# Stage borders, first loads and closing rows of a two-block transformer kernel, changed together

## The reference

```python
def reference(x, c, ctx, ...):
    x = first_block(x, c, ctx, ...)        # attention + mLSTM mixer, then 16 experts
    return second_block(x, c_2, ctx_2, ...)  # two layers

# first_block: x = x + g1 * mixer(modulate(rmsnorm(x)))    8-head latent attention, a bidirectional mLSTM
#              x = x + g2 * ec_moe(modulate(rmsnorm(x)))   each expert takes 128 tokens; scatter-add
#              return rmsnorm(x, final_norm)
# _layer of second_block, for l in (0, 1):
shift, scale, gate = split(silu(c) @ w_mod + b_mod, 3)
h  = _rmsnorm(x, norm_g) * (1 + scale) + shift
parts = _split_cols(h @ w_in)              # q, k, v, gates, Fourier, convolution and pooling inputs
o_att = silu(parts[3]) * _latent_attention(q, k, v, kc, vc)   # 4 query heads, 2 key heads of width 64
out = concatenate([o_f, o_att, o_c, o_p]) @ w_out
x_new = x + gate * out                     # the context rows too, in layer 0
```

## Time and profile before

| | |
|---|---|
| median of 3 runs | 3560.42 us (3559.0 to 3563.74) |
| the profiled execution | 3564.75 us |
| its span, first to last instruction | 3563.0 us |
| PE busy | 3214.0 us, 90% |
| DVE / ACT / POOL busy | 52% / 40% / 20% |
| mean granted PE clock | 0.946 of full |

### The profile page before, as it was taken

The page is one execution under the profiler, slowest core; times in us unless marked ns, Lnnn a source line. Parts: engine busy times, 40 slices in busy tenths (PEclk is TensorE's granted clock), DMA queues, the critical chain, the costliest instruction groups (busy, mean ns, idle before and its releaser), DMA issues. The chain is left out here.

```text
span 3563.0 us, 43053 instructions
## 1 busy us (share of the span) xinstructions
PE 3214.0 (90%) x17109; PEld 2595.1 (73%) x17109; DVE 1852.6 (52%) x2501; ACT 1413.5 (40%) x1941; POOL 695.1 (20%) x460
## 2 busy tenths in 40 slices
PE   7989998999999799793999999599988996998989
PEld 3867775778778677673878787488877775887867
DVE  4366785444444354646788888434416443152643
ACT  4222231433333244432777777431116434212640
POOL 2200001011111255200455555220001003000100
PEclk7999999999999899896999999799999997999999
DMA  6426555001000231324999999421112134211122
GB/s 200 117 80 209 182 170 184 31 24 44 24 26 24 59 116 58 131 103 184 359 378 388 379 389 372 143 66 52 38 34 54 48 113 154 61 43 44 48 72 83
DMA packets 247250, 470.72 MB, mean 132 GB/s; under 512 B 23936, under 2 KB 135673, under 8 KB 247053
## 3 DMA queue, kind: packets, MB, share of 16 engines
q1 hardware_dynamic: 231304, 410.09, 33.4%
q0 software_dynamic: 15264, 57.70, 4.9%
q10 hardware_dynamic: 484, 0.15, 0.0%
HBM read 405.34 MB, written 55.22 MB: 129 GB/s over the span
## 5 line engine op out<-in xcount | busy, mean ns | idle before, releaser
L2558 DVE TENSOR_TENSOR exp_wl<-wts_raw,exp_wh 128x2048 fp32r<-128x2048 f32 x144 | 394.3, 2773 | 105.9 <-ACT exp_wh L2518 105.9
L2518 ACT ACTIVATE exp_wh<-wts_raw 128x2048 fp32r<-128x2048 f32 x192 | 368.0, 1919 | 196.5 <-PE exp_gate L2447 64.1
L2724 PE MATMUL pr_ps<-l_h_high,pr_wh 128*128 128x512 f32 (+1 forms) x896 | 335.1, 374 | 0.0
L2725 PE MATMUL pr_ps<-l_h_low,pr_wh 128*128 128x512 f32 (+1 forms) x896 | 329.6, 368 | 0.0
L2726 PE MATMUL pr_ps<-l_h_high,pr_wl 128*128 128x512 f32 (+1 forms) x896 | 329.0, 367 | 0.0
L2417 POOL TENSOR_TENSOR exp_wl<-wts_raw,exp_wh 128x2048 fp32r<-128x2048 f32 x48 | 229.4, 4780 | 265.0 <-ACT exp_wh L2518 265.0
L842 PE MATMUL in_ps<-iw_h_high,in_wh 128*128 128x512 f32 (+1 forms) x696 | 268.7, 386 | 0.0
L843 PE MATMUL in_ps<-iw_h_low,in_wh 128*128 128x512 f32 (+1 forms) x696 | 263.8, 379 | 0.0
L844 PE MATMUL in_ps<-iw_h_high,in_wl 128*128 128x512 f32 (+1 forms) x696 | 263.3, 378 | 0.0
L2886 DVE TENSOR_TENSOR pr_wl<-pw_raw,pr_wh 128x512 fp32r<-128x512 f32 x84 | 57.7, 691 | 333.4 <-ACT pr_wh L2804 332.1
L1067 DVE SCALAR_TENSOR_TENSOR g_scratch<-g_scratch,g_c 128x512 f32<-128x512 f32 x240 | 181.8, 785 | 19.8 <-DVE g_scratch L1067 12.7
(11 more groups left out here) (515 smaller groups left out, 7222.8 us busy)
## 6 DMA issues: line engine op xcount, KB each, us to landing
wts_raw<-in_w_e_gate SPq DMA_DIRECT2D x64, 1024.0 KB, 9.6
wts_raw<-in_w_e_up SPq DMA_DIRECT2D x64, 1024.0 KB, 8.8
wts_raw<-in_w_e_down SPq DMA_DIRECT2D x64, 1024.0 KB, 7.6
g_scratch<-in_w_mod SPq DMA_DIRECT2D x80, 512.0 KB, 4.6
pw_raw<-in_w_in SPq DMA_DIRECT2D x88, 256.0 KB, 2.9
iw_raw<-in_w_in SPq DMA_DIRECT2D x74, 256.0 KB, 4.6
mod_w<-in_w_mod SPq DMA_DIRECT2D x4, 2048.0 KB, 11.7
wo_w<-in_w_out SPq DMA_DIRECT2D x2, 4096.0 KB, 13.6
```

The lines of the kernel that those rows point to most:

```text
L2518: act.activation(wh[:, m % RING], raw[:, m % RAW_RING], ACT.Copy).then_inc(high, 1)
L2558: dve.tensor_tensor(wl[:, m % RING], raw[:, m % RAW_RING], wh[:, m % RING].bitcast(F32), ALU.subtract).then_inc(low, 1)
L2724: nc.tensor.matmul(out, wh[:, slot, k, :], hi, start=h == 0 and k == 0, stop=False)
L2725: nc.tensor.matmul(out, wh[:, slot, k, :], lw, start=False, stop=False)
```

## The change

- `Phase` takes a phase `to`. With it, its semaphores are handed on and neither cleared nor followed by a barrier at its end. A carrier phase `g.carry` collects them; they are cleared where iw, mli, mw, pw0, pw1 and wo1 end. A new phase `two` around both layers holds the weights ring, its semaphores and those of `project_out`'s stores. mod, iw, mli, mw, pw0, pw1 and wo1 still end with a clearing and a barrier.
- All Blocks are opened with `no_gpsimd_drain=True`.
- `project_first`: two row buffers used in turn; five quarters a tile at first and four from the 70th, so that block 19 falls to the last tile instead of behind it; the gates are copied, turned and added three to five tiles after `xm` 7, inside the loop, in the buffer `kr`.
- `FinalRows`: context rows in two loads; x1 before the table; the first weights are issued by ACT, which waits for the last scatter first.
- `project_in`: ACT rounds the keys after tiles 17 and 18, DVE takes their rests after 19 and 20, POOL zeroes the other half; they lie in a buffer that `attention_2` uses directly.
- `attention_2`: SP only prefetches the Fourier operands. Queries are rounded from `parts` for two row tiles at a time (three ACT and two DVE instructions), the first pair ahead of the loop, the next in each second unit. POOL has no list any more.
- `project_out`: the last tile is multiplied and finished by column halves; a tile's norm comes ahead of the preparation of later tiles; SP issues the next layer's first four half tiles of weights at the end of its list; with a normed copy POOL doesn't wait for the stores.
- `TurnedRows` with loads: SP loads row by row tile, each behind the store of that tile, the 7th and later ones behind all stores of xb; ACT and DVE start behind all stores.

```diff
 class Phase(ExitStack):
+    def __init__(self, nc, tag, to=None):
     def __exit__(self, *exc):
         if exc[0] is None:
-            self.nc.clear_and_free_semaphores(self.sems)
-            self.nc.all_engine_barrier(sem_only=True)
+            if self.to is not None:
+                self.to.sems += self.sems
+            else:
+                self.nc.clear_and_free_semaphores(self.sems)
+                self.nc.all_engine_barrier(sem_only=True)
...
-        with nc.Block() as block:
+        with nc.Block(no_gpsimd_drain=True) as block:
...
 class TurnedRows:
     def sync(self, sp, also):
-        for n, (src, t) in enumerate(self.pairs):
-            if self.x_in:
-                sp.dma_start(self.x[:, 2 * n:2 * n + 2, :], ...).then_inc(self.x_in[n], 16)
-            if n == 0:
-                also(sp)
+        if self.x_in:
+            for n, src in enumerate(self.rows_of):
+                sp.wait_ge(self.g.xn_stored[n % 2], 16 * (n // 2 + 1))
+                if n == ROWS_FREE:
+                    for j in range(2):
+                        sp.wait_ge(self.g.xb_stored[j], 16 * self.g.n_xb[j])
+                sp.dma_start(self.x[:, n, :], src).then_inc(self.x_in[n], 16)
+        also(sp)
...
 class FinalRows:
     def sync(self, sp, also):
-        sp.dma_start(self.x[:, 0:CT, :], g.io["ctx_2"]...).then_inc(self.ctx_in, 16)
+        for n in range(CT):
+            sp.dma_start(self.x[:, n, :], g.io["ctx_2"][n * P:(n + 1) * P, :]).then_inc(self.ctx_in[n], 16)
         sp.dma_start(self.fn, spread(g.io["final_norm"])).then_inc(self.fn_in, 16)
-        also(sp)
         sp.wait_ge(g.scattered, 16 * N_EXP)
         for n in range(LT):
             sp.dma_start(self.x[:, CT + n, :], g.x1[n * P:(n + 1) * P, :]).then_inc(self.x_in[n], 16)
+        also(sp)
...
 def quarter_counts():
-            done += 1 if name == "xm" else 4 if done < 26 or i >= len(FIRST) - 4 else 3
+            done += 1 if name == "xm" else 5 if done < 28 else 4 if done >= 70 else 3
...
 def project_first(nc, g):
-                    if n:
-                        act.wait_ge(row_out, 32 * n)
+                    if n >= 2:
+                        act.wait_ge(row_out[n % 2], 32 * (n // 2))
+                    mrow = mrows[n % 2]
...
+                    if i == GATES_OUT + 1:          # PE; ACT at GATES_OUT, DVE at GATES_OUT + 2
+                        pe.wait_ge(grow_ready, 3)
+                        for q in range(4):
+                            mm = pe.transpose(gacc[:, q * 96:(q + 1) * 96], grow[:, q * P:(q + 1) * P], ...)
...
 def project_in(nc, g, l, last, streams, flat):
+                if not last:
+                    act.wait_ge(g.scattered, 16 * N_EXP)
+                    first_weights(act)
...
+                def round_key(j):
+                    for side in range(2):
+                        act.activation(key_high[j][side * HD:(side + 1) * HD], g.parts[j * HD:(j + 1) * HD, K_AT, :],
+                                       ACT.Copy).then_inc(key_rounded, 1)
+                    if i in (17, 18):
+                        round_key(i - 17)
...
 def attention_2(nc, g, l, last, prefetch):
-                act.wait_ge(raw_in, 32)
-                act.activation(kh[:, 0, :], raw[:], ACT.Copy).then_inc(high, 1)
-                act.wait_ge(q0_in, 32)
-                act.activation(q[:, 0, lo:], src[:, lo:], ACT.Copy).then_inc(high, 1)
+                def round_queries(s):
+                    j, cols = two_tiles(s)
+                    src = g.parts[:, Q_AT + j, cols]
+                    act.activation(q[0:HD, 2 * j, cols], src[0:HD], ACT.Copy).then_inc(q_rounded, 1)
+                    act.activation(q[HD:, 2 * j + 1, cols], src[HD:], ACT.Copy).then_inc(q_rounded, 1)
+                    act.activation(q[0:HD, 2 * j + 1, cols], src[HD:], ACT.Copy).then_inc(q_rounded, 1)
+                round_queries(0)
...
                         copy_four(u, "e0")
+                        if splits(u):
+                            round_queries(u // 2 + 1)
                         copy_four(u, "e1")
...
 def project_out(nc, g, l, jobs, normed=None):
+                if normed is not None:
+                    for m in range(HALF_RING):
+                        half_tile(sp, g, l + 1, m)
...
-                    if normed is not None:
-                        pool.wait_ge(xn_out[j], 8 * len(tiles))
...
+                    if n == end:
+                        for c in range(2):
+                            three_terms_half(nc, acc[:, n % 2], ..., c).then_inc(multiplied, 1)
...
+                        for c in range(2):          # DVE, last tile
+                            dve.wait_ge(multiplied, n + 1 + c)
+                            dve.tensor_tensor(y[:, j, cols], acc[:, j, c], gate[:, s, cols], ALU.mult)
+                            dve.tensor_tensor(y[:, j, cols], y[:, j, cols], x[:, j, cols], ALU.add)
```

341 lines of the change are left out of this document (196 added, 145 removed).

## The result

The changed kernel takes 3520.19 us (median of 4 runs, 3516.36 to 3523.28) where the kernel before, run beside it, takes 3559.93 (4 runs, 3559.0 to 3563.74): a ratio of 0.9886, 95% interval 0.9871 to 0.9901, so 39.7 us faster. The time lies inside the range, 8.2 us above the forecast.

The account below looks back on a forecast made before the run. PE, busy 90% of the span, was taken as the bound, so only its stops could be won. Terms 4.4 + 4.8 + 8.6 + 10.0 + 8.4 + 11.2 + 1.1 = 48.5 off 3564.75, then 4.33 for the median, gave 3512; range 3499 to 3532.

Parts of the forecast that it names:

- End of project_first: Stage end: last block comes with the last tile, gates done in the loop, SP starts 4.9 earlier; 4.4 us gained.
- Borders: Stage borders: 12 clearings with their barriers go away at 0.4 each; 4.8 us gained, bounds 0 and 6.4.
- Experts to the first projection: Border behind the experts: without POOL's drain SP loads earlier and ACT squares earlier; 8.6 us gained, bounds 5 and 10.
- ACT waits for the scatter (2278.1): Behind the experts: scatter lands 6.1 after issue, ACT then issues four weight loads and squares from 2280.2 instead of 2286.24.
- Rival 1: Borders behind the experts and between layers: POOL's queue is still awaited, losing 5.0 and 2.8; 3520 us, chance 0.13.
- Attentions: Starts of both attentions: turned values and e0 turn come earlier; 10.0 us gained in the first, 8.4 in the second.
- e0: Attentions' starts: PE's first turn of the exponential's result, ending the chain forecast 10.0 us shorter, 8.4 in the second.
- Rival 2: Attentions: queries' roundings on ACT aren't hidden, 1.0 for each of 16 pairs, 16 us lost; 3528 us, chance 0.11.
- First to second projection: Border between the layers: earlier last store, SP start and first row tile; 11.2 us gained, bounds 9 and 12.5.
- Roundings of the keys, quarters: Keys' roundings moved into the projection, and five quarters a tile in project_first: each put at 0 cost beside PE-bound tiles.
- Rival 4: project_first: DVE's added quarters meet POOL's multiplications, two tiles lose 2.38 each, 4.8 together; 3517 us, chance 0.08.
- rival 3: Attentions: a rounding between exponentials makes ACT reload its function, 4.2 a pair, 67 us lost; 3579 us, chance 0.03.

Follow-up runs that it names:

- drains_back: Changed kernel, but every Block ends with POOL's drain again, semaphores still handed on; 3530.68 us, ratio 0.9917.
- old_pace: Changed kernel with the earlier kernel's pace of quarters (four a tile at first, then three, four at the end), gates still inside the loop; 3523.09 us.
- gain_late: Changed kernel, but SP issues the first weights, ACT doesn't wait for the scatter, and the final norm's gain loads behind x1's first tile; 3520.84 us.
- ctx_late: Changed kernel, but SP waits for the experts' last scatter before it loads the context rows; 3518.16 us, ratio 0.9888.
- clear_each: Changed kernel, but every phase clears its own semaphores at its end again, Block ends still without a drain; 3521.55 us, ratio 0.9893.
- keys_late: Changed kernel, but ACT and DVE round the keys at the attention's start instead of in the projection; 3531.13 us, ratio 0.9908.
- whole_tile: Changed kernel, but the closing tile of both project_out stages is multiplied and finished whole again; 3520.11 us, ratio 0.9882.
- rows_late: Changed kernel, but SP loads layer 1's row tiles only when all stores of the first project_out have landed; 3519.86 us, ratio 0.9882.
- best: Changed kernel with gain_late's edits, and POOL rounding the queries of all later pairs and taking their rests; 3509.18 us, ratio 0.9860.
- query_long: Changed kernel, but queries for the pair following the short (context) units are rounded in the last long unit before them; 3518.17 us, ratio 0.9884.

## Why the prediction was right, and where not

The direction, the places and most prices held. What was off is the sum: 48.5 forecast, 41.5 in the profiles. Beside it the changed kernel's profile stands only 3.1 above its median, not the 4.33 assumed; that makes the 8.2.

- *End of project_first*, 4.4 forecast, 5.1 measured, 4.7 at SP's start. The size is right, and that is partly luck. The prediction takes the transfers issued at 591.63 for the last ones and lets the gates' end set SP's start; a further pair of transfers and POOL's drain come behind both, to 600.23. The drain, which was not named here, is the larger part (2.7 of the 4.7, 2.1 of the stretch by drains_back). The gates had to go as well: without the drain they would have ended last, only 0.87 ahead of its end; that is worked out from these instants and not shown by a run. That the last block comes with the last tile was named as a cause and is none (old_pace).
- *Borders*, 0.4 for each clearing: right. Before against after, the borders between plain stages are 0.3 to 0.7 shorter with one clearing less (at readout's start only 0.02) and 0.7 with two. The 2.3 of the six borders in the table agrees by luck, since 1.9 of it lies in the first block's attention, whose length varies by more. Taking the drain away does nothing at a plain border (drains_back).
- *Experts to the first projection*, 8.6 forecast, 6.4 measured: the step that failed is "ACT waits for the scatter (2278.1)". It kept the scatter's 6.1 of before, where nothing was beside it. Loads that start in the same moment make it 10.1; 8.3 with less beside it, 6.1 without (gain_late, ctx_late). The step ahead of it, "SP starts near 2274.0", was off too: that is 2.1 after the scatter's issue, and SP starts 0.07 after it. With the loads 2.4 after the issue the scatter still lands at 6.1 (clear_each), so the early start of SP and the late scatter belong together. The Trainium skill, "DMA: Bandwidth & Descriptors", section "Queues, rings and completion order", states that each DMA engine takes turns between the queues that have work for it, a packet at a time. The trace agrees with it only in part: from 2271.2 on packets of both queues run, but for 4.1 us ahead of that the loads' alone, and in clear_each it is the loads that wait. Why the scatter's first packet comes so late is not shown. Rival 1, POOL's queue still awaited at the border, did not come about: SP starts 1.5 before POOL's issue ends.
- *Attentions*, 10.0 and 8.4 forecast for the first chain. That was right: the e0 turns come 10.1 and 8.2 earlier after PE's entry, and with the roundings taken off ACT the stages are 12.1 and 8.9 shorter than before. The failed step is "I take 0" for the queries' roundings. A copy of 64 x 256 was held to be a quarter of one of 128 x 512; it takes 0.41 and not 0.14, so three take 1.2, more than the 1.00 of idle time. Half the partitions save nothing: a copy of 64 x 1280 takes the 1.27 that one of 128 x 1280 took in the kernel before (keys_late). By these rows (0.41, 0.60 and 1.27 for 256, 512 and 1280 columns) a copy costs near 0.2 us and 0.85 ns for each column, which is an estimate. Most units absorb the copies, as the unit behind is half a microsecond shorter (4.27 instead of 4.74); the first units of the first attention and those around the short units don't. Rival 2 was thus right in kind and at 4.7 instead of 16 in size.
- *First to second projection*, 11.2 forecast: counted from PE's last product of the first project_out, PE's first turn comes 10.75 earlier (9.16 instead of 19.91) and the first product 11.3 (36.1 instead of 47.4). The mechanism held step by step (store 4.45 after PE's last product, forecast 4.7; first tile landed 9.1 after it, forecast 9.5; whole_tile and rows_late take back 2.0 and 1.9). Only the last store lands later than forecast, 9.8 after that product instead of 7.8. The stretch shows 8.3 because the second projection, behind its first product, loses 2.4 against the kernel before, 0.7 at its start and 1.7 at the place shown in the last section. That is the clock: PE has the lower one for 37.5 us of this stage, 33.1 in the kernel before, and for 29.7 to 30.5 in the five variants in which the stage takes 292.0 to 292.2.
- *Last tile* 1.1: right, 1.1 by whole_tile, from PE's last product to the end.
- *Roundings of the keys, quarters* at 0: right by keys_late and old_pace; the prefetch, also at 0, has no run of its own. Rival 4, DVE against POOL in project_first, and rival 3, a function reload in each pair, are not there: in both attentions together ACT reloads twice, once at each start.

The Fourier stages give 3.2 where 1.6 was forecast. The first takes 42.7 in the changed kernel, and 44.3 to 44.4 in six variants with the same instructions there, so 1.7 of it are such a difference between executions. Left open: what holds the scatter's first packet back, what POOL's drain does behind a store that has landed, and the landing of the second x1 tile in `best`.

## What to carry to other kernels

A start that a change pulls forward runs beside what it used to follow: before pricing it, list the transfers still under way at that moment and price them beside the new ones, here 4 us on a scatter that two engines wait for, and nothing where the loads came 2.4 us behind it. Work that goes into another engine's idle time must be priced at the smallest tile's own duration, not as a share of a larger one, and the idle time read in the first and the odd units as well as in the steady ones. An engine without any work in a stage can be the place for such pieces: on POOL they cost the first attention 4 us less than on ACT.

## What the runs showed of the hardware

The same instructions in the same order were granted different clocks in different executions. The rows below are from the merge, which no edit touches (columns: stretch, length, busy time of PE, PEld, DVE, ACT and POOL, granted clock, DMA share, GB/s); the first two are the changed kernel, the others query_long.

```profile
1515.00:1520.00 5.00, 4.26 (x29) 3.80 (x29) 2.60 (x3) 3.34 (x6) 0.00 (x0) 0.89 0.48 168
1520.00:1525.00 5.00, 5.00 (x13) 3.84 (x13) 4.36 (x8) 1.69 (x4) 1.06 (x2) 0.50 0.16 65
```

```profile
1513.00:1518.00 5.00, 4.26 (x32) 3.70 (x31) 2.45 (x2) 2.98 (x4) 0.00 (x0) 1.00 0.60 209
1518.00:1523.00 5.00, 5.00 (x23) 4.04 (x23) 4.20 (x7) 1.84 (x5) 1.05 (x2) 1.00 0.06 21
```

In the second 5 us PE is busy throughout, and its granted clock is 0.50, the lower of the two levels (1.2 of 2.4 GHz), in the one execution and full in the other. In the 5 us ahead of it PE is idle for the same 0.74 in both. The whole stage takes 178.8 in the first execution and 175.6 in the second. The second projection has such a place too. In the changed kernel the clock falls during 32 products of two columns each and stays at 0.50 for 6.8 us; in the kernel before it falls behind the same products, for 3.4 us; in ctx_late it stays full, and the stage is 3.4 shorter than in the changed kernel. The rows are a timeline and two stretches of the changed kernel, and one stretch of the kernel before.

```profile
3045.89 4.83 PE L145 MATMUL pr_ex<-g_block,l_parts 128*128 128x2 f32 x32
...
3048.00:3050.00 2.00, 2.00 (x12) 2.00 (x11) 0.35 (x1) 0.00 (x0) 0.00 (x0) 0.52 0.00 0
...
3052.00:3054.00 2.00, 2.00 (x3) 0.62 (x2) 0.69 (x1) 0.00 (x0) 0.00 (x0) 0.50 0.00 0
```

```profile
3084.00:3086.00 2.00, 2.00 (x6) 0.99 (x4) 1.19 (x2) 0.00 (x0) 0.00 (x0) 0.54 0.02 4
```

The stage takes 292.0 to 293.2 in seven of the 13 profiles and 295.4 to 295.6 in the other six, whatever the edit. A handful of such places, each at 1.7 to 3.5 us, would be enough for the 5 to 10 us by which executions of one kernel differ here; only the profiled execution of each kernel can be read so, so that is not shown for the others.
